# Low halves of the second block's up tiles: made by VectorE, or by a transfer that adds the raw tile onto its negated high half

## What is computed

```
    u = rms_norm(h, norm_mlp_pre[l])
    hid = jnp.square(jax.nn.relu(jnp.einsum("btd,df->btf", u, w_up[l])))
    m = jnp.einsum("btf,fd->btd", hid, w_down[l])
    h = h + rms_norm(m, norm_mlp_post[l])
```

## Time and profile before

| | us |
|---|---|
| median of 3 runs | 1020.32 |
| lowest and highest | 1019.99, 1020.34 |
| span of the profiled execution, first to last instruction | 1018.8 |
| TensorE busy in it | 1010.3 (99%) |
| VectorE busy | 758.5 (74%) |
| ScalarE busy | 556.8 (55%) |
| GpSimd busy | 232.6 (23%) |

### The profile page before, as it was taken

One profiled execution on the slowest core, in us unless ns is written; L12 is line 12 of the kernel. 1 busy time (PEld: TensorE's weight loads), 2 busy tenths in 40 slices (PEclk: granted clock), 3 DMA queues, 4 the chain that ended last, 5 costly groups with the idle time before them and its releaser, 6 DMA issues.

```text
span 1018.8 us, 14751 instructions
## 1 busy us (share of the span) xinstructions
PE 1010.3 (99%) x5688; PEld 851.1 (84%) x5688; DVE 758.5 (74%) x1208; ACT 556.8 (55%) x848; POOL 232.6 (23%) x322
## 2 busy tenths in 40 slices
PE   9999999999999999999999999999999999999997
PEld 6877788888888877788888888998888888888886
DVE  6997568788777887578787778888865457766665
ACT  6575566545556466656554556845544455334433
POOL 0572600000000272800000004019947620000000
PEclk9999999999999999999999999999999999999999
DMA  9641545555554351365554544553445556564541
GB/s 362 232 159 59 176 155 207 190 182 207 194 180 173 114 218 42 125 221 193 212 195 177 207 168 163 171 201 119 170 150 184 204 186 227 191 214 174 182 149 41
DMA packets 27894, 180.24 MB, mean 177 GB/s; under 512 B 3120, under 2 KB 3248, under 8 KB 7472
## 3 DMA queue, kind: packets, MB, share of 16 engines
q1 hardware_dynamic: 27824, 179.30, 49.5%
HBM read 178.24 MB, written 1.05 MB: 176 GB/s over the span
## 4 chain that ended last, share of the span: by engine, by line
PE 97%; DVE 1%; ACT 1%; DMA 0%; issue 0%; SPq 0%; DVEq 0%
PE pb L747 17%; PE pb L752 10%; PE pb L609 9%; PE pb L610 9%; PE pb L612 8%; PE pb L772 6%; PE pb L771 6%; PE pb L773 6%; PE pb L754 3%; PE pb L1017 2%; PE pb L970 2%; PE pb L673 1%; PE pb L672 1%; PE pb L674 1%; PE pb L709 1%; PE pb L985 1%
## 5 line engine op out<-in xcount | busy, mean ns | idle before, releaser
L1895 DVE TENSOR_TENSOR wlo<-raw,whi 128x2048 fp32r<-128x2048 f32 (+1 forms) x125 | 282.8, 2265 | 102.4 <-ACT whi L1374 102.2
L1374 ACT ACTIVATE whi<-raw 128x2048 fp32r<-128x2048 f32 x159 | 298.5, 1881 | 60.5 <-PE pb L612 34.6
L2772 POOL TENSOR_TENSOR wlo<-raw,whi 128x256 fp32r<-128x256 f32 x268 | 206.8, 810 | 318.9 <-ACT whi L1374 315.2
L747 PE MATMUL pb<-hb,whi 128*128 128x512 f32 x770 | 183.7, 389 | 0.0
L747 PEld LDWEIGHTS pb<-hb,whi 128*128 128x128 f32 x770 | 144.6, 188 | 30.4
L609 PE MATMUL pb<-whi,hb 128*128 128x512 f32 x336 | 134.2, 399 | 0.1
L610 PE MATMUL pb<-wlo,hb 128*128 128x512 f32 x336 | 130.9, 390 | 0.0
L612 PE MATMUL pb<-whi,hb 128*128 128x512 f32 x320 | 124.9, 390 | 0.0
L752 PEld LDWEIGHTS pb<-hb,wlo 128*128 128x128 f32 x880 | 112.8, 191 | 4.3
L752 PE MATMUL pb<-hb,wlo 128*128 128x256 f32 x880 | 114.2, 283 | 0.0
L772 PE MATMUL pb<-wlo,gh 128*128 128x512 f32 x280 | 109.2, 390 | 0.0
(11 more groups left out here) (404 smaller groups left out, 1558.8 us busy)
## 6 DMA issues: line engine op xcount, KB each, us to landing
raw<-wst SPq DMA_DIRECT2D x159, 1024.0 KB, 4.8
raw<-wst SPq DMA_DIRECT2D x10, 512.0 KB, 4.3
gb<-gains SPq DMA_DIRECT2D x3, 512.0 KB, 6.4
XN<-xt SPq DMA_DIRECT2D x2, 512.0 KB, 5.3
X<-x SPq DMA_DIRECT2D x1, 1024.0 KB, 12.1
out<-X SPq DMA_DIRECT2D x4, 256.0 KB, 2.0
PQ<-prm SPq DMA_DIRECT2D x1, 909.0 KB, 4.5
raw<-wst SPq DMA_DIRECT2D x2, 256.0 KB, 7.3
```

The source lines that it names most:

```text
L747: e.matmul(b[:, :], wh[:, k, s], hb2[:, k, :, :].rearrange("p i q -> p (i q)"), start=k == 0, stop=False)
L1374: e.activation(whi[:, split_slot(m), 0:w], raw[:, m % RAW, 0:w], ACT.Copy).then_inc(*hi(m))
L1895: e.tensor_tensor(wlo[:, split_slot(m), s], raw[:, m % RAW, s], whi[:, split_slot(m), s].bitcast(F32), ALU.subtract).then_inc(*lo_v(m))
L2772: g = e.tensor_tensor(wlo[:, split_slot(m), s], raw[:, m % RAW, s], whi[:, split_slot(m), s].bitcast(F32), ALU.subtract)
```

## The change

For up tiles 2 to 15 of the second block (14 tiles, named in `by_dma`) VectorE no longer makes the low half. ScalarE writes a second copy behind the high half: raw times minus one, rounded in the same way, into the low half's place. GpSimd waits for it (`minus_hi`) and issues a transfer that adds the raw tile onto it. The transfer's landing (`low_landed`, on two semaphores in turn) is what TensorE's low products wait for, and what SP's load into that raw buffer waits for. Up tiles 0 and 1 and all down tiles stay as they were.

```
+        by_dma = [tile_at[2, "up", j, 0] for j in range(2, 16)]
...
+        s_low = [sem(f"s_low{i}") for i in range(2)]
+
+        def low_landed(m):
+            j = by_dma.index(m)
+            return s_low[j % 2], 16 * (j // 2 + 1)
...
         def lows(m):
 
+            if m in by_dma:
+                return (low_landed(m),)
             return (lo_g[m], lo_v[m]) if low_shared(m) else (lo_of(m)[m],)
...
                 q.wait_ge(*ready[7])
-                q.wait_ge(*lo_of(m)[m])
+                for low in lows(m):
+                    q.wait_ge(*low)
...
                     e.activation(whi[:, split_slot(m), 0:w], raw[:, m % RAW, 0:w], ACT.Copy).then_inc(*hi(m))
+                    if m in by_dma:
+                        e.activation(wlo[:, split_slot(m), 0:w], raw[:, m % RAW, 0:w], ACT.Copy, scale=-1.0).then_inc(*minus_hi(m))
...
-                if m is None or on_pool(m):
+                if m is None or on_pool(m) or m in by_dma:
                     return
...
             root("post1")
             m = ahead_to(m, 2, "down", 15, 0)
+            for m in by_dma:
+                q.wait_ge(*minus_hi[m])
+                e.dma_start(wlo[:, split_slot(m), :], raw[:, m % RAW, :], accum_op=ALU.add).then_inc(low_landed(m)[0], 16)
             root("post2")
```

More of the change, by code:

```diff
@@ L331, in program @@
         (hi, squares, diag, hh_done, proj0, qk_a, gate_exp, relu, tanh_h, exped, pt_a, last_v, ce_turned, mix_hh, act,
-         ff_low, ff_cc, ff_tanh, gh_done, gated, normed_a) = act_all = signals(
+         ff_low, ff_cc, ff_tanh, gh_done, gated, normed_a, minus_hi) = act_all = signals(
             SQ, "hi squares diag hh_done proj0 qk_a gate_exp relu tanh_h exped pt_a last_v ce_turned mix_hh act "
-                "ff_low ff_cc ff_tanh gh_done gated normed_a")
+                "ff_low ff_cc ff_tanh gh_done gated normed_a minus_hi")
         (lo_v, x_new, mean_sq, hl_done, proj1, roped, qk_v, zeroed, pos_done, scored, cmp_v, maxed, normed, selected,
```

## The result

The changed kernel takes 1036.95 us (median of 4 executions, 1035.91 to 1037.45) against 1020.21 for the kernel before: a ratio of 1.0162, 95% interval 1.0148 to 1.0177. It is **16.7 us slower**. The forecast was 12.4 us slower. The profiled span is 1035.6 us against 1018.8, 16.8 more, so the trace holds nearly all of the loss.

What follows compares the result with a forecast made beforehand. TensorE, busy 165.00 of 165.00 us in the loop, was taken as the bound; 1.2 us at tile 2 plus 11.2 over twelve tiles on the 1018.8 us span, with 1.5 to the median, gave 1032.7 us, range 1019.8 to 1062.

Steps and rivals of the forecast that it cites:

- The bound and the place: In the changed loop TensorE is never idle; VectorE's freed 32 us are worth nothing, waits come only before line 761's low products.
- Tile 2: First transferred up tile: lands 7.3 us after the negated copy against a window of 6.1 us, so TensorE waits 1.2 us.
- Two passes of 5.0 us: Adding transfer on the DMA engines: two reads per byte written, 5.0 us of moving, landing after 7.3 us when alone.
- GpSimd's issue inside the 4.8 us: GpSimd's issue of a transfer was taken as SP's, already inside a load's 4.8 us from issue to landing.
- The collision: In the loop two loads, 5.0 us of moving, run beside each transfer, which lands after 12.3 us, over its 10.25 us window.
- if both queues share equally: On the DMA engines, 5.0 us of adding beside 5.0 us of loading take 10.0 us, plus 2.3 us fixed.
- An even 0.93 us in twelve steps: Up tiles 3 to 14: each low half late by 0.93 us, the step growing from 11.0 to 11.9 us, 11.2 us together.
- a raw tile lands some 0.6 us ahead of its own high half's start: Loads in the loop: at half share a load takes 7.3 us, landing 0.6 us before ScalarE needs it; loads nearly bind.
- The load of ScalarE: Fourteen added copies of 1.92 us, 27 us, cost nothing: 3.5 us of cover before the next `gh`.
- Tile 15: Last transferred up tile meets only one load and lands after 9.8 us, within 10.25 us, so no wait.

Runs made afterwards that it cites:

- The plain transfer: The changed kernel with the addition left out of its fourteen GpSimd transfers, so they are plain moves of the same tiles: 1022.33 us, ratio 1.0023.
- half loads: The changed kernel with every load from up tile 3 on moving only the first half of its tile: 1028.66 us, ratio 1.0081.
- the kernel with three stalls: The changed kernel with only tiles 4, 8 and 12 by transfer, each issued after 5, 7 or 9 scratch subtractions on GpSimd: 1031.49 us, ratio 1.0110.

## Why the prediction was right, and where it was not

**The bound and the place: right.** TensorE was full in the loop, no other line waits, and what VectorE got back was worth nothing.

**Tile 2: right.** Forecast 7.3 us from the negated copy's end and 1.2 us late. The copy ended at 851.15, the low products began at 858.63, 7.5 us later, and waited 1.21 us. Alone, the loss was measured too (the kernel with tile 2 only).

**Two passes of 5.0 us: right.** 5.2 us of engine time, packets of about double length. The plain transfer lands in 4.4 us alone, the adding one in 7.1: the difference, 2.7 us, is close to the 2.5 us that one pass was priced at. That the second pass is the second read fits this, but no run shows what is done in it. The Trainium skill's rule ("Collectives: The Full Stack", The bandwidth ceiling: two source reads, no cycles for the add itself) agrees in kind; the 4.2 us estimated from its rate are below the 5.2 measured.

**GpSimd's issue inside the 4.8 us: right.** The plain transfer lands 4.4 us after issue, where SP's load takes 4.8. GpSimd is busy 0.88 us for each issue, which delays nobody. The 0.4 us more that the Trainium skill ("DMA: Bandwidth & Descriptors", Specifications) gives to the first byte of such a transfer do show in the first packet: at tile 2 it comes 1.32 us after issue for the plain transfer and 1.62 for the adding one, against 0.95 for a load alone (issued at 851.50 in the kernel before). They do not show in the landing.

**The collision: right in size, wrong in kind.** The step that failed is "if both queues share equally". A transfer issued between 2.2 us after and 0.7 us before two whole loads starts some 3.6 us later than one alone (5.1 to 5.4 us to its first packet against 1.4 to 1.6). That is half of its delay or more; its moving then takes 6.3 to 8.2 us, where equal sharing forecast 10.0. The landing of 11.9 to 14.0 us is near the forecast 12.3, so the landing does not tell the two mechanisms apart; the order of the packets does, 5.4 us in which none of the transfer's moved.

**An even 0.93 us in twelve steps: wrong.** The working assumed that the loads follow every late landing in the same way. In fact a load issued into the crowd takes 10.4 us, not the 7.3 taken from half share; over the 26 loads of the loop the median is 8.0 us and the longest 13.4. The forecast "a raw tile lands some 0.6 us ahead of its own high half's start" failed, and ScalarE waited 2.5 to 2.9 us for a raw tile three times. That wait moves the next transfers out of the crowd. On average the two patterns cost about the same: 16.3 - 5.1 = 11.2 us by the steps, against 1.2 + 11.2 = 12.4 forecast. That is luck: nothing in the working gives 2.2 us in every third step.

**The term that was missing: TensorE's clock, 5.1 us.** The sum took every product at full clock and did not ask what a stall does to it. Of four stalls of 1.9 to 2.5 us three were followed by 3.41 us at 1.2 GHz; an even 0.9 us would perhaps not have been, as eight stalls of up to 1.4 us with half loads were not. This term makes up more than the whole of the 4.3 us by which the forecast fell short.

**The load of ScalarE: right, with a condition.** "This costs nothing" holds in the changed kernel, because VectorE loses its subtraction at the same time. With VectorE's subtraction kept behind the copy, 1.2 us appear.

**Tile 15: right.** No wait stands ahead of its low products.

**Open.** Why a transfer's first packet waits even for loads that were issued up to 0.7 us after it: the trace shows the order of the packets, not what the DMA engines had queued. And which stall lowers the clock: over all kernels, seven of nine stalls of 1.89 us and more did, but one of 2.00 and one of 3.09 us did not, so their length alone does not decide it. Nor is the number of falls the same each time: of the four executions of the kernel with three stalls, two with a mean granted clock of 0.996 took 1030.55 and 1030.93 us, two with 0.994 took 1032.07 and 1032.06. One fall of 3.41 us makes 0.0017 of that mean. And no run frees the loads from waiting for a transfer, so that this wait calls up the collision is read from the issue times alone.

## What to carry to other kernels

A DMA queue with half its time free can still be unable to take another transfer on a deadline: look at when the other transfers are issued, since an adding transfer issued beside two loads of 1 MB landed here after some 12 to 14 us in place of 7. Handing a buffer's release to such a transfer also ties the loads to it (one landed at 872.34, the load went out at 872.41), so the new transfer calls up its own collision; asking less of it (every other tile, or half of each) cost nothing that could be measured here, and gained nothing either. Where TensorE is the bound, price a stall of 2 us at nearly 4, as here a stretch at half clock mostly followed it.

## What the runs showed of the hardware

- An adding transfer moves 8 KB packets in 0.63 us, a plain one of the same queue in 0.325 us, a load in 0.31 us; 1 MB alone lands 7.1 us and 4.4 us after GpSimd's issue.
- The first packet of a transfer that GpSimd issues comes 1.4 to 1.6 us after the issue when it is alone (1.1 to 1.3 without the addition), and 4.3 to 5.8 us after when two whole loads went out between 2.2 us before and 0.7 us after it, adding or not; with half loads 3.1 to 5.6. In that time 95 to 224 load packets went by. A load alone has its first packet 0.95 us after SP's issue.
- A transfer already under way holds up loads that start beside it: one took 10.4 us, against 4.8 us in the kernel before. A transfer that started late is slowed as well: 6.3 to 8.2 us of moving in place of 5.2.
- TensorE at half clock (granted 0.50) for 3.41 us after stalls of 1.89, 2.19, 2.25, 2.28, 2.44 and 2.49 us, and for 6.83 us around one of 4.24 us; none after stalls up to 1.8 us, nor after one of 2.00 and one of 3.09 us.
